# The MLP of a hybrid decoder layer by a 2x2x2 block scheme of seven products instead of eight

## The reference

```python
x = x + rms_norm(merged.astype(x.dtype) @ lp['w_out'], lp['norm_post_mix'])
h2 = rms_norm(x, lp['norm_pre_mlp'])
ff = jnp.square(jax.nn.relu(h2 @ lp['mlp_w1'])) @ lp['mlp_w2']
x = x + rms_norm(ff, lp['norm_post_mlp'])
```

## Time and profile before

| | |
|---|---|
| median of 3 runs | 2088.18 us (2088.11 to 2091.5) |
| the profiled execution | 2088.61 us |
| its span, first to last instruction | 2087.0 us |
| PE busy | 2006.5 us, 96%, 13822 matmuls |
| PEld, DVE, ACT, POOL busy | 91%, 46%, 26%, 32% |
| granted TensorE clock, mean | 0.989 |
| moved by DMA | 223.5 MB, mean 107 GB/s |

### The profile page before, as it was taken

How to read it: one execution, slowest core, us unless ns; L and a number is a source line. 1 busy time by engine, 2 the same in 40 slices (tenths; PEclk the granted TensorE clock), 3 DMA queues, 4 the chain that set the end, 5 groups by cost and what they waited for, 6 DMA issues and landing times.

```text
span 2087.0 us, 32964 instructions
## 1 busy us (share of the span) xinstructions
PE 2006.5 (96%) x13822; PEld 1905.8 (91%) x13822; DVE 957.1 (46%) x1320; ACT 541.5 (26%) x815; POOL 666.7 (32%) x352
## 2 busy tenths in 40 slices
PE   4999999999999998998999999899999999999997
PEld 4999899999998995777999999899999999999996
DVE  7894441245444425664345737852313232222327
ACT  4211211243343326674110134320101010010102
POOL 1222111111111113442556621223434344343453
PEclk9999999999999999999999999999999999999998
DMA  3433436566667533322354333301111111111132
GB/s 127 103 97 105 108 96 181 162 203 199 202 217 225 189 130 94 93 62 93 101 188 142 124 99 101 99 23 50 41 52 41 51 41 48 45 43 49 41 134 84
DMA packets 151478, 223.50 MB, mean 107 GB/s; under 512 B 34576, under 2 KB 108560, under 8 KB 151344
## 3 DMA queue, kind: packets, MB, share of 16 engines
q1 hardware_dynamic: 139248, 193.42, 30.2%
q10 hardware_dynamic: 12096, 28.12, 3.7%
HBM read 173.84 MB, written 45.56 MB: 105 GB/s over the span
## 4 chain that ended last, share of the span: by engine, by line
PE 91%; DVE 5%; ACT 2%; issue 1%; DMA 1%; POOL 0%; SPq 0%; POOLq 0%; DVEq 0%; ACTq 0%
PE ps L1817 70%; PE ps L2013 3%; PE ps L2113 2%; PE ps L2040 2%; PE ps L2052 2%; PE ps L2205 2%; PE ps L1837 1%; PE ps L1956 1%; PE ps L2137 1%; PE ps L1918 1%; PE ps L1937 1%; PE ps L2182 1%; PE ps L1905 1%; PE ps L1945 1%; PE ps L1901 0%
## 5 line engine op out<-in xcount | busy, mean ns | idle before, releaser
L747 POOL TENSOR_TENSOR w_hi<-w_raw,zeros 128x1024 fp32r<-128x1024 f32 x78 | 190.2, 2439 | 531.3 <-PE ps L1817 460.7
L1817 PE MATMUL ps<-op_hi,w_hi 128*128 128x352 f32 x1536 | 345.3, 333 | 8.7 <-DVE op_lo L1544 4.8
L739 POOL TENSOR_TENSOR w_lo<-w_raw,w_hi 128x1024 fp32r<-128x1024 f32 x54 | 133.6, 2474 | 652.6 <-ACT w_hi L840 652.6
L1817 PE MATMUL ps<-op_lo,w_hi 128*128 128x352 f32 x1536 | 334.0, 326 | 0.0
L1817 PE MATMUL ps<-op_hi,w_lo 128*128 128x352 f32 x1536 | 332.1, 324 | 0.0
L1817 PEld LDWEIGHTS ps<-op_hi,w_hi 128*128 128x128 f32 x1536 | 260.3, 189 | 20.3 <-issue 14.2
L1817 PEld LDWEIGHTS ps<-op_lo,w_hi 128*128 128x128 f32 x1536 | 263.4, 189 | 0.0
L1817 PEld LDWEIGHTS ps<-op_hi,w_lo 128*128 128x128 f32 x1536 | 262.1, 189 | 0.0
L749 POOL TENSOR_TENSOR w_lo<-w_raw,w_hi 128x1024 fp32r<-128x1024 f32 x78 | 203.5, 2610 | 6.1
L1817 PE MATMUL ps<-hid_hi,w_hi 128*128 128x352 f32 x816 | 176.8, 325 | 4.0 <-DVEq L1707 2.3
L1817 PE MATMUL ps<-hid_lo,w_hi 128*128 128x352 f32 x816 | 177.7, 326 | 0.0
(11 more groups left out here) (301 smaller groups left out, 3049.2 us busy)
## 6 DMA issues: line engine op xcount, KB each, us to landing
w_raw<-in_w SPq DMA_DIRECT2D x148, 512.0 KB, 3.7
kc<-in_k_cache SPq DMA_DIRECT2D x48, 448.0 KB, 5.2
vc<-in_v_cache SPq DMA_DIRECT2D x48, 448.0 KB, 6.6
out_keep<-stage ACTq DMA_DIRECT2D x24, 528.0 KB, 2.7
tmp_gate_d<-stage ACTq DMA_DIRECT2D x24, 528.0 KB, 4.6
gate_t<-tmp_gate_d SPq DMA_DIRECT2D x24, 528.0 KB, 3.7
qkv<-out_keep SPq DMA_DIRECT2D x15, 512.0 KB, 4.6
acc<-in_x SPq DMA_DIRECT2D x8, 528.0 KB, 6.7
```

Of the source, the lines that this page charges most:

```text
L739: pool.tensor_tensor(w_lo[:, b].rearrange("p k m -> p (k m)"), w_raw[:, b], w_hi[:, b].rearrange("p k m -> p (k m)").bitcast(F32), ALU.sub ...
L747: pool.tensor_tensor(hi.rearrange("p (a m) -> p a m", a=2), w_raw[:, b].rearrange("p (a m) -> p a m", a=2), zeros[:].unsqueeze(1).broadcas ...
L1817: mm = pe.matmul(ps[:, 3 * dst + q, 0:BLK], w[:, b, w0 + n], x[:, k, q * BLK:(q + 1) * BLK], start=(n == 0 and part == 0), stop=(n == len( ...
```

## The change

The scheme (a form of Strassen's with fewer additions) splits k, output and tokens in two each. For an up unit (one chunk): k 1024 in two of 512, output 512 in two of 256, tokens 1056 in two of 528. Four quadrants of weights (11, 12, 21, 22) and of tokens, sums s1 to s4 of weights, t1 to t4 of tokens; seven products ("entries") in place of eight, whose results are added up into four blocks. The up units of chunks 2 to 7 and all down units go this way, down units by twos (`SUPER`, k 1024). Chunks 0 and 1 are multiplied up as before.

An entry of the array is `strassen`, 4*2*3*2 = 48 matmuls of 264 tokens into four banks; a down product j is two entries (u = 0, 1). Weight quadrants are loaded as 512 KB blocks of their own. Three weight slots rotate; their high parts are now made by ACT (`entry_high`), low parts and weight sums by POOL. DVE adds PSUM to the hidden rows, squares them with relu (the norm's factor is now multiplied into the token operand before the products, `x_norm`, from x2 loaded again from DRAM as `xq`), and makes the t sums. The seven operand blocks of each up unit are stored to DRAM (`h_d`) and loaded again for the down products (`t_load`), split there into high (ACT) and low (DVE). The hidden rows of chunks 0 and 1 are stored too (`hp_d`), and `job` makes their sums from them at the start of the down part. In the down part DVE adds each product to one of seven sums, and at the end combines them into four blocks; the last two products run by quarters of 264 tokens.

The semaphores of earlier stages are used again, each with the count it was left at (`Resumed`, `past`). The launch and the order of weights in DRAM are the same. The diff, cut to its core:

```diff
+UP_ORDER = [("11", "11"), ("s1", "t1"), ("s2", "t2"), ("s3", "t3"), ("s4", "22"), ("12", "21"), ("22", "t4")]
+DOWN_ORDER = [("11", "11"), ("s2", "t2"), ("s3", "t3"), ("22", "t4"), ("s1", "t1"), ("s4", "22"), ("12", "21")]
+def past(eng, r, n):
+
+    if n > 0:
+        eng.wait_ge(r.sem, r.left + n)
...
+            sy.wait_ge(w_split[1], P_MLP + 4)
+            up_quad(0, "22")
+            plain_store(6)
+            past(sy, rows_dead, 1)
+            up_quad(0, "21")
+            up_quad(0, "12")
+            plain_store(7)
...
+                for name in ("22", "t3"):
+                    t_store(g, name)
+                if g == JOB - 1:
+                    past(sy, entry, E_DOWN - 2)
+                    for n in range(2):
+                        past(sy, t_out[n], 16 * (5, 2)[n] * 2)
+                    t_load(0)
+                    past(sy, entry, E_DOWN - 1)
+                    down_quad(0, 1, "11")
+                    t_load(1)
+                    down_quad(0, 1, "21")
+                    down_quad(0, 1, "22")
+                for name in ("11", "t1", "t2"):
+                    t_store(g, name)
+            past(sy, entry, E_DOWN)
+            down_quad(0, 1, "12")
+            t_store(JOB - 1, "21")
+            t_store(JOB - 1, "t4")
...
+            JOBS = {1: second_job, 3: lambda: t_stores(JOB + 1)}
+            job_load(0)
...
+                        t_load(j + 2)
+                    if n == 0:
+                        JOBS.get(i, nothing)()
...
+                        past(sy, t_low, NP * len(SUPER))
+                        past(sy, w_low, E_ALL - 3)
+                        for k in range(KD):
+                            sy.dma_start(res_rows[k][:], t["x2_d"][:, k]).then_inc(x2_in, 16)
...
+                low(e, q["11"])
+                past(pool, quad_in[g % 2]["22"], 16 * (g // 2 + 1))
+                past(pool, quad_in[0]["21"], 16 * (g + 1))
+                past(pool, w_low, e - NP + 5)
+                total(q["s1"], q["21"], q["22"], ALU.add)
+                past(pool, w_sum, n + 1)
+                total(q["s2"], q["s1"], q["11"], ALU.subtract)
+                low(e + 1, q["s1"])
+                past(pool, w_sum, n + 2)
+                total(q["21"], q["11"], q["21"], ALU.subtract)
+                low(e + 2, q["s2"])
+                past(pool, quad_in[0]["12"], 16 * (g + 1))
+                past(pool, w_low, e + 2)
+                total(q["s1"], q["12"], q["s2"], ALU.subtract)
+                past(pool, w_sum, n + 4)
+                low(e + 3, q["21"])
+                low(e + 4, q["s1"])
+                low(e + 5, q["12"])
+                low(e + 6, q["22"])
...
+            past(act, h_out, 16 * STD)
+            past(act, x_low, NP)
+            for e in range(E_ALL):
+                past(act, entry, e + 1 if e < E_ALL - 2 * 2 else 0)
+                if e < E_DOWN:
+                    g, i = e // NP, e % NP
+                    if i < 2:
+                        keep(g, ("11", "22")[i], e % 2)
+                if e + 3 < E_ALL:
+                    entry_high(e + 3)
+                if e == E_DOWN - 3:
+                    t_high_part(0)
+                if e == E_DOWN - 1:
+                    t_high_part(1)
+                if e >= E_DOWN and e % 2 and (e - E_DOWN) // 2 + 2 < NP * len(SUPER):
+                    t_high_part((e - E_DOWN) // 2 + 2)
...
+            x_norm("11")
+            x_norm("22")
+            std_unit(2)
+            x_norm("12")
+            x_norm("21")
+            x_low_part("11", "11")
+            dve.wait_ge(mm_ready[0], USES[P_MLP] + 2)
+            x_low_part("22", "22")
+            x_sum("22", "22", "12", ALU.subtract, 4)
+            std_unit(3)
...
+            for name, src in (("t3", "22"), ("21", "21"), ("t4", "12")):
+                x_low_part(name, src)
...
+            for g in range(len(UPS)):
+                e, m = NP * g, NP * g
+                ps_add(e + 2, g, "12", "11")
+                past(dve, t_out[1], 16 * 2 * g)
+                ps_add(e + 3, g, "21", "12")
+                tt(o_t["12"], o_t["12"], o_t["22"], ALU.add)
+                tt(o_t["22"], o_t["22"], o_t["21"], ALU.add)
+                square_of(o_t["22"]).then_inc(t_made.sem, 1)
+                ps_add(e + 4, g, "12", "12")
+                step(square_of(o_t["12"]))
+                past(dve, t_made, m + 1)
+                v.tensor_tensor(o_t["t3"], o_t["22"], o_t["12"], ALU.subtract).then_inc(t_made.sem, 1)
+                ps_add(e + 5, g, "11", "11")
+                if g == JOB - 1:
+                    t_low_part(0)
+                square_of(o_t["11"]).then_inc(t_made.sem, 1)
+                past(dve, t_made, m + 3)
+                v.tensor_tensor(o_t["t1"], o_t["12"], o_t["11"], ALU.subtract).then_inc(t_made.sem, 1)
+                v.tensor_tensor(o_t["t2"], o_t["t3"], o_t["11"], ALU.add).then_inc(t_made.sem, 1)
+                ps_add(e + 6, g, "21", "21")
+                square_of(o_t["21"]).then_inc(t_made.sem, 1)
+                past(dve, t_made, m + 6)
+                v.tensor_tensor(o_t["t4"], o_t["21"], o_t["t2"], ALU.subtract).then_inc(t_made.sem, 1)
+            t_low_part(1)
...
+                    if j + 2 < NP * len(SUPER):
+                        t_low_part(j + 2)
+                    if n == 0 and i in (0, 2):
+                        job(i // 2)
+                    if last and i:
+                        past(dve, kept_dve, K0 + 2 * j + 2)
+                        past(dve, combined, i - 1)
+                        combine(*((1, 0), (2, 1), (3, 2), (1, 4))[i - 1])
...
+            past(dve, w_low, E_ALL - 2)
+            dve.wait_ge(x2_in, 16 * KD)
+            for q in range(LAST_P):
+                for x in range(4):
+                    add_last(q, x)
...
+            def strassen(e, op, bank):
+
+                w_h, w_l = slot(e)
+                for k in range(FCH):
+                    for m in range(2):
+                        for part, (w, y) in enumerate(((w_h, op[0]), (w_h, op[1]), (w_l, op[0]))):
+                            for z in range(2):
+                                mm = pe.matmul(ps[:, 4 * bank + 2 * m + z, 0:QUART], w[:, FCH * m + k], y[:, k, z * QUART:(z + 1) * QUART],
+                                               start=(k == 0 and part == 0), stop=(k == FCH - 1 and part == 2))
+                return mm
...
+                    if e < 2:
+                        te.wait_ge(mm_free[e], USES[P_MLP] + FCH)
+                    elif (e - 2) % NP < 2:
+                        past(te, kept_act, 2 * ((e - 2) // NP) + (e - 2) % NP + 1)
+                    else:
+                        past(te, kept_dve, 5 * ((e - 2) // NP) + (e - 2) % NP - 1)
+                    strassen(e, up_op[name], e % 2).then_inc(entry.sem, 1)
...
+                            past(te, w_low, e + 1)
+                            past(te, kept_dve, 5 * len(UPS) + 2 * (j - 1) + u + 1)
+                            strassen(e, down_op[j % 2], u).then_inc(entry.sem, 1)
```

More of the change, by code:

```diff
@@ new lines, in up_source, with down_source @@
+        def up_source(g, name):
+            return q22_odd if name == "22" and g % 2 else q_b[0][sum_of(name)]
+        def down_source(u, name):
+            return q_b[u][{"s3": "21", "s4": "s2"}.get(name, name)]
+        o_t = {"11": stage[:, 0], "22": stage[:, 1]}
+        for n, name in enumerate(("12", "21", "t2", "t3", "t4")):
+            o_t[name] = at("R", n * ROW, "o_" + name, [P, N])[:]
+        o_t["t1"] = o_t["12"]
+        sums = [at("A", n * KH, f"sum{n}", [P, FCH, HALF]) for n in range(4)] + [at("R", n * KH, f"sum{n + 4}", [P, FCH, HALF]) for n in range(3)]
@@ new lines, in t_high_part, with keep @@
+            def t_high_part(j):
+                past(act, t_raw_in[j % 2], 16 * (j // 2 + 1))
+                past(act, entry, E_DOWN + 2 * (j - 1) if j >= 2 else E_DOWN - NP + 2 + j)
+                s.activation(down_op[j % 2][0][:].rearrange("p k n -> p (k n)"), t_raw[j % 2][:].rearrange("p k n -> p (k n)"),
+                             ACT.Copy).then_inc(t_high.sem, 1)
+            def keep(g, name, x):
+                past(act, t_out[0], 16 * 5 * g)
+                s.activation(four(o_t[name]), banks(x), ACT.Copy).then_inc(kept_act.sem, 1)
@@ L1747, in _, with x_norm @@
-            last = u1 + (NCH - 2) * per
-            for n in range(FCH):
-                hidden(FCH * (NCH - 1) + n, n, 1, last)
-            sums(last + 2)
+            def x_norm(name):
+                k0, half = (0, FCH)[name[0] == "2"], int(name[1]) - 1
+                for k in range(FCH):
+                    mm = v.scalar_tensor_tensor(out=xq[name][:, k], in0=xq[name][:, k], scalar=gains[:, 2, k0 + k:k0 + k + 1],
+                                                in1=pre_rstd[:, half * HALF:(half + 1) * HALF], op0=ALU.mult, op1=ALU.mult)
+                mm.then_inc(x_made.sem, 1)
@@ new lines, in _, with square_of @@
+            x_low_part("t1", "12")
+            std_unit(4)
```

(18 more changed lines are left out.)

596 lines of the change are left out of this document (436 added, 160 removed).

## The result

The changed kernel takes 2097.98 us (median of 6 runs, 2094.89 to 2099.25), the kernel before 2088.95 (2088.11 to 2091.5): a ratio of 1.0039, 95% interval 1.0028 to 1.0049. It is slower by 9.0 us. The forecast was 2107, slower by 19; the time lies within its range and on its side, at a little under half its size.

What follows compares the result with a forecast made beforehand. The array (PE) was taken as the bound; -72 array, -3 gaps, +9 start, +16.5 periods, +36 passage, +4 bursts, +26 end, +3 clock gave +19.5, about 2107 us; range 2066 to 2130, the forecast's own 2085 to 2128.

Steps and rivals of the forecast that it cites:

- The wait for DVE's sum ahead of each up unit's second entry: Up units: DVE's sum of entry 6 comes behind operations alternating with POOL, leaving the array 3.3 us idle per unit.
- the late loads behind t3's store: Up-to-down passage: SP issues the first operand load only after t3 is stored, so j=0 starts at 48.9 instead of 41.6.
- the copies behind the jobs: Passage: the plain unit's four differences run to 94, so the sum j=2 needs ends at 95.5 against 85.
- stands 16.5 and 36: Predicted array idle: 16.5 us over five up-unit periods, and 36 us in the passage from up to down.
- I take 123.8, between two bounds: Step of a 264-column matmul: 123.8 ns, between 121.8 (extra scales with columns) and 125.7 (extra fixed); an entry 5.94 us.
- bursts +4: Steady down units: 4 us of array idle for POOL's bursts at the start of each of three rounds.
- two waits on which the end hangs add some 3: Last part: the granted clock falls where the array idles, and two waits there add some 3 us to the span.
- -75 and +94.5: Gains: array -72, gaps -3. Losses: start +9, periods +16.5, passage +36, bursts +4, end +26, clock +3.
- A: Rival: DVE and POOL alternate more weakly, the array binds the up units, and the kernel takes 2067 us; chance 0.20.
- B: Rival: short matmuls have hardly an extra, 264 columns take 0.113 us, and the kernel takes 2080 us; chance 0.08.
- C: Rival: loading 128x128 weights keeps matmuls from shortening, a step is 0.14 us, and the kernel takes 2160 us; chance 0.05.
- D: Rival: DRAM traffic makes loads come some us later per unit, and the kernel takes 2130 us; chance 0.07.

Runs made afterwards that it cites:

- e1: In the up loop DVE adds the seventh product's PSUM pair ahead of the two sums making t1 and t2, against the changed kernel: 2079.75 us.
- e2: Changed kernel with POOL making one column instead of 1024 of each weight sum in the later up units, part of the computation left out: 2080.48 us, one run.
- e3: Changed kernel with SyncE issuing the first three operand-block loads at the up-to-down passage ahead of waiting stores: 2084.70 us.
- e8: Four-moves kernel, with ACT instead of DVE copying the first down super-tile's 14 PSUM pairs and load 4 ahead of the first job's stores: 2051.71 us.
- e4: Changed kernel with the eight residual-row loads issued as places come free, and DVE waiting for them only ahead of the second last piece: 2098.56 us.
- four moves: Changed kernel with seventh sum ahead of t1 and t2, passage loads ahead of stores, residual rows early, ACT's first copy not behind x low parts: 2064.64 us.

## Why the prediction was right and wrong

Its steps, against the trace of the kernel after:

| | forecast | measured |
|---|---|---|
| tile 4 starts | 1364.0 | 1365.7 |
| entry 2 starts | 1432.9 | 1432.8 |
| period of an up unit | 44.9 | 44.3; 45.0 as the mean of five from entry 2 |
| j=0 starts | 1694.4 | 1694.7 |
| j=0's second half, j=1 | 1706.5, 1718.5 | 1706.0, 1717.2 |
| the pair that j=2 needs | 1741.0 | 1742.0 |
| j=4 starts | 1770.5 | 1770.3 |
| E, j=25 ends | 2036 | 2029.7 |
| hole in the last part | 14 | 14.1 |
| end, from E | 66.5 and 3 for the clock | 67.2 |

**Up to j=4, 405 us of changed code, the forecast was 0.2 us off. The causes were right; that the sum came out so near is luck.** The wait for DVE's sum ahead of each up unit's second entry, its cause, the late loads behind t3's store, the copies behind the jobs, and DVE as the bound of the last part were all as told; e1, e2, e3, e8 and e4 show each. The sizes were not. In us, a stand here without the one matmul step (0.12) in it, and the low clock as what is left, the half clock behind stands:

| stretch | forecast | measured |
|---|---|---|
| entry 2 to j=4 | 48 entries 285.1, stands 16.5 and 36: 337.6 | 279.7, stands 11.8 and 30.2, low clock 15.8: 337.5 |
| j=4 to E | 44 entries 261.4, bursts 4: 265.4 | 256.4, a stand 1.2, low clock 1.8: 259.4 |
| E to the end | 66.5, clock 3: 69.5 | 67.2 |

Up to j=4 two errors and one omission cancel: the stands were 10.5 us less, the entries 5.4 less, and the half clock behind the stands, which the forecast put at nothing in the up units and in the passage, costs 15.8. It can be read from the trace apart from this remainder: four entries behind a stand took 1.6 us more each, at 0.77, and j=0's two entries ran at 0.80 and 0.73 with their stands in them. So a unit's 3.3 us of idle were 2.5 and 1.6 of clock, with seven entries some 0.8 us shorter.

**The steps that failed are sizes, and from j=4 on nothing cancels them.** First, "I take 123.8, between two bounds": where the clock is full the step was 121.4 ns, just under the lower bound of 121.8, in which the extra scales with columns; over the 2112 matmuls to E that is 5.0 us. Second, "bursts +4": one stand of 1.2, less 2.8 us; on the other side stand 1.8 of low clock behind j=4's stand, not in the forecast here. Third, "two waits on which the end hangs add some 3": the clock did fall there (0.67 from 2050.8 to 2060, 0.74 from 2070 to 2085), but DVE, busy for 13.7 of those last 15 us, sets the pace, and from E to the end it is 67.2 us for 66.5 without the term. With the 0.2 up to j=4 this adds up, within rounding, to the 8.6 us between spans of 2105.5 and 2096.9. The size of the change missed by half because it is a small difference of large terms, -75 and +94.5.

The rivals: A's time, 2067, is what the kernel reaches with four moves (2064.64), but by order and not by a weaker alternation. Its criterion, the sum of entry 6 within 5.9 us of the entry, is what e1 meets. B's 0.113 and C's 0.14 are both refuted by 0.1214; C's cause may be real below 264 columns, where the step stays at 0.112 with 216. D: no steady down unit waited for a load.

One part of the trace is no more than scatter: a stand in the output projection, in code that none of the experiments touches, began between 1303.35 (e1) and 1308.93 us (e8). Differences of profiles are therefore taken here from stretch to stretch.

## What to carry to other kernels

When a change gives two engines work that excludes each other, write their streams out in time and look at what stands ahead of the operation the array waits for: here one line moved ahead of two that nobody waited for turned +9 us into -10, and the whole set of moves into -41. Work that feeds only a store belongs behind what frees PSUM (unless, as with t4 at the passage, the array soon waits for what that store sets off), and loads whose data are ready belong ahead of stores that wait. Moving an operation forward also moves its own wait forward, and with it everything behind.

## What the runs showed of the hardware

- A stand of 2.5 us of the array was followed, four times in five, by an entry at a mean clock of 0.77: 7.4 us for 5.8. Where that happened it added some 60% to the price of the stand.
- 132 columns with a weight load each ran at a granted clock of 0.50 from 1500 to 2380 us, 0.2138 us a step, though PE was busy for 100.00 of 100 us; 216 columns had 1.00 and 0.1121 where nothing was waited for. What between them decides is open.
- The SBUF-only DVE operations of 1056 that make t1 and t2 took 3.3 to 3.45 us beside POOL's and 1.25 without them (e2); those with a PSUM operand 1.24 to 1.26 in both. The Trainium skill, "SBUF — State Buffer", section "SBUF: two separate sides", calls the pair of ports that both use an exclusive lock, held for a whole instruction; the trace agrees.
- The last transfer that a chain of waits names may have a bound right behind it: 9.45 us of DMA were worth 1 us of stand (e4).
